# A two-block language-model forward pass: the expert passes' row places in five pieces, and two weight pieces behind the merged rows

## The chip, the cores and the metric

The kernel runs on one core of a Trainium2 chip. The metric is the device time of one execution in microseconds (us). Three runs of the kernel before gave 2496.23, 2499.69 and 2502.55 us; the median is 2499.69 us.

## The reference

The input is 256 tokens of width 1024. Two blocks of two layers each run one after the other, and everything is computed in fp32. In the first block each layer norms the rows, runs four token mixers (retention, a state-space scan, gated linear attention, an mLSTM) on slices of one wide projection, and merges them; then comes a feed-forward part, dense in layer 1 and with eight experts in layer 2. The second block (layers 3 and 4) has other mixers and dense feed-forward parts. Cut to what the change touches:

```
ybr = jnp.stack([y_ret, y_ssd, y_gla, y_ml], axis=2)
gates = jax.nn.sigmoid(mgate.reshape(bsz, seq, N_BRANCH, D_MODEL))
merged = jnp.sum(gates * jnp.einsum('bsnv,nvd->bsnd', ybr, w_branch), axis=2)
return merged @ w_out                       # 1024 x 1024
...
top_vals, top_idx = lax.top_k(logits, TOP_K)          # TOP_K = 2 of 8 experts
...
for e in range(N_EXPERTS):
    out = out + gate[..., e:e + 1] * ((silu(h @ w1[e]) * (h @ w3[e])) @ w2[e])   # 1024 -> 2816 -> 1024
```

## The kernel before, in words

**Weights in two parts.** Every large product is made of three matmuls in a reduced fp32 format: high part of the rows by high part of the weights, low by high, high by low (`split_product`, lines 955 to 957). Weights come by DMA into two ring slots and a third one, on the queue of SyncE. They are then cut into pieces of 128x1024. For each piece ScalarE writes the high part `w_hi` (line 1787, in the experts line 1954), VectorE subtracts it from the weights and writes the low part `w_lo` (line 2811; for the mixers' gate weights GpSimd does it), and TensorE multiplies. There are four places for pieces (`NPIECE`): ScalarE can fill a place when TensorE is done with the piece four before. A ring slot comes free for the next transfer when the low parts of all its pieces are made.

**The order of work.** There is no scheduler. Each engine's program is written out by hand, is executed in that order, and semaphores tie the engines together. An engine that waits holds back all that stands behind it.

**End of the mixers in layers 1 and 2** (`L` 0 and 1). The 1024x1024 output weights are eight pieces, M+40 to M+47, where M is the first piece after the head's. VectorE adds the last gated branch into `merged` (lines 2294 and 2297, eight instructions). TensorE turns the merged rows in four steps into four PSUM banks (line 911), ScalarE copies each to the high part of the rows (`hT_hi`, line 1807), VectorE makes each low part (`low_rows`, in `merged_low`, through line 2811) and with it gives the bank free. The first output product writes one bank per half of the tokens, and these two are the banks of the first two steps: so it starts when two low parts of rows are made. In VectorE's program before, the low parts of pieces M+42 and M+43 stand between the last add and the low parts of the rows.

**The experts** (`experts`). Tokens are sorted to experts, at most 128 to a pass; a pass takes one expert's weights. In this case eight passes run. A pass gathers its rows by matmul, goes through 11 chunks of 256 hidden columns (the loop over `c`, 0 to 11; chunk `c` has four pieces of gate and up weights, and two of the down weights of chunk `c`-1), and the next pass scatters the rows back by a matmul with `selT`. For one chunk VectorE makes six low parts of weights, the low part of the turned hidden rows (`fhT_lo`) and the product of gate and up (line 3020, which the trace calls `u_z`). TensorE's transposes of the hidden rows wait for that product.

At `c` = 1 and 2 VectorE also makes half of the next pass's gather matrix (`select_places`, lines 2949 and 2950). At `c` = 4 it makes all of the scatter matrix and weight of the pass (`places_back`, lines 2999 to 3008): two comparisons of 128x256, their sum, a sum over the row, `selT`, and the next slot number. The trace names their memory `gates`. Each of these waits for the one before it by the semaphore `sel_step`. What it makes is read by the scatter at the start of the next pass.

Of the kernel before, what the change touches and what calls it, by code (L numbers as in the profile page):

```python
# [21 lines left out]
ALU = mybir.AluOpType  # L22
ACT = mybir.ActivationFunctionType
AX = mybir.AxisListType

P = 128
STEP, LINE = 8, 16
T = 2
# [131 lines left out]
HEAD_PIECES = sum(CHUNK_PIECES[:6])  # L160
# [97 lines left out]
def build(nc, a, out):  # L258
# [7 lines left out]
    with ctx:  # L266
# [10 lines left out]
        def sem(name):  # L277
            return ctx.enter_context(nc.semaphore(name))
# [32 lines left out]
        with ExitStack() as expert_rows:  # L311
            selT = expert_rows.enter_context(nc.sbuf_tensor("selT", [P, S], F32R))
# [82 lines left out]
        slot_no, slot_weight = g1[:, 324:325], g1[:, 325:326]  # L395
        quad_b = g0[:, 0:4 * S].rearrange("p (q s) -> p q s", q=4)
        sel = g0[:, 4 * S:5 * S].rearrange("p (t s) -> p t s", t=T)
        slot_rows, slot_rows2 = g0[:, 5 * S:6 * S], g0[:, 6 * S:7 * S]
# [6 lines left out]
        def const2(name):  # L405
# [70 lines left out]
        both_ready, count_mm, rank_mm, quad_ready, quad_out, quad_in, table_ready = (sem(s) for s in (  # L476
            "both_ready", "count_mm", "rank_mm", "quad_ready", "quad_out", "quad_in", "table_ready"))
        sel_ready, gather_mm, xg_ready, selT_ready, scatter_mm, ys_ready = (sem(s) for s in (
            "sel_ready", "gather_mm", "xg_ready", "selT_ready", "scatter_mm", "ys_ready"))
# [33 lines left out]
        MIX, FFN = [0] * 4, [0] * 3  # L513
# [16 lines left out]
        for key, m in PC.of.items():  # L530
            if key[0] != "ffn" and key[:-1] + (key[-1] + 1,) not in PC.of:
                L, job = key[0], key[1:-1]
# [114 lines left out]
        for l in range(2):  # L647
            L = 2 + l
# [1498 lines left out]
        def _(v):  # L2147
            tt, ts, stt, cp = nc.vector.tensor_tensor, nc.vector.tensor_scalar, nc.vector.scalar_tensor_tensor, nc.vector.tensor_copy
# [197 lines left out]
            def mixers(L):  # L2346
# [12 lines left out]
                M = M0 + HEAD_PIECES  # L2359
# [23 lines left out]
                for n in range(4):  # L2383
# [4 lines left out]
                         in1=ea[:, L].unsqueeze(1).to_broadcast([P, T, 4]), op0=ALU.mult, op1=ALU.mult))  # L2388
# [114 lines left out]
                head_norm(L, 3, 2, u_gla[:, :, 4 + MW:], False)  # L2503
                low_range(M + 40, M + 42)
                merge(L, 3)
                low_range(M + 42, M + 44)

            def normed(src, n_g, cols, gcol, m, r, w):

# [300 lines left out]
            def low(dst, src, hi):  # L2810
                return tt(dst, src, hi.bitcast(F32), ALU.subtract)  # L2811

            def low_range(lo, hi):

                for m in range(lo, hi):
                    v.wait_ge(w_hi_ready, m + 1)
                    low(w_lo[:, m % NPIECE], source[m][0], w_hi[:, m % NPIECE]).then_inc(w_split, 1)
# [128 lines left out]
            def select_places(step, tiles=range(T)):  # L2946

                for i in tiles:
                    step(ts(sel[:, i], const("iota"), place[:, 0, i:i + 1], None, ALU.is_equal))
                    ins = stt(out=sel[:, i], in0=const("iota"), scalar=place[:, 1, i:i + 1], in1=sel[:, i], op0=ALU.is_equal, op1=ALU.add)  # L2950
                    if i < T - 1:
                        step(ins)
                    else:
                        ins.then_inc(sel_ready, 1)

            def experts():
                route()
                select_places(link)
                pass_table()
                n_pass = passes(v)  # L2960

                def rows_low(passed):

                    for h in range(2):
                        cols = slice(h * 512, (h + 1) * 512)
                        v.wait_ge(ys_hi_ready, 2 * passed + h + 1)
                        ins = stt(out=ys_lo[:, cols], in0=mb[h][:], scalar=slot_weight, in1=ys_hi[:, cols].bitcast(F32),
                                  op0=ALU.mult, op1=ALU.subtract)
                    ins.then_inc(ys_ready, 1)

                with v.Fori(0, n_pass) as t:
                    n = [0]
                    STEPS = 9

                    def step(ins):
                        n[0] += 1
                        ins.then_inc(sel_step, 1)
                        v.wait_ge(sel_step, t * STEPS + n[0])

                    def low_parts(lo, hi):  # L2980
                        for m in range(lo, hi):
                            c, q = PIECE_LIST[m]
                            v.wait_ge(e_hi_ready, t * ALL_PIECES + m + 1)
                            low(w_lo[:, m % NPIECE], expert_piece(c, q), w_hi[:, m % NPIECE]).then_inc(e_split, 1)

                    def gathered(half):
                        v.wait_ge(xg_hi_ready, 2 * t + half + 1)
                        low(xg_lo[:, 4 * half:4 * half + 4], mb[2 + half][:].rearrange("p (k s) -> p k s", k=4),
                            xg_hi[:, 4 * half:4 * half + 4]).then_inc(xg_ready, 1)

                    at = 4
                    low_parts(0, 1)
                    gathered(0)
                    low_parts(1, 2)
                    gathered(1)
                    low_parts(2, 4)
                    rows_low(t)

                    def places_back():
                        v.wait_ge(quad_in, 16)  # L3000
                        v.wait_ge(scatter_mm, T * (t + 1))
                        step(stt(out=slot_rows, in0=quad_b[:, 0], scalar=slot_no, in1=quad_b[:, 2], op0=ALU.is_equal, op1=ALU.mult))
                        step(stt(out=slot_rows2, in0=quad_b[:, 1], scalar=slot_no, in1=quad_b[:, 3], op0=ALU.is_equal, op1=ALU.mult))
                        step(tt(slot_rows, slot_rows, slot_rows2, ALU.add))
                        step(nc.vector.tensor_reduce(slot_weight, slot_rows, AX.X, ALU.add))
                        ts(selT[:], slot_rows, 0.0, None, ALU.is_gt).then_inc(selT_ready, 1)
                        v.wait_ge(selT_ready, t + 2)
                        step(ts(slot_no, slot_no, float(P), None, ALU.add))

                    for c in range(NF + 1):  # L3010
                        if c:
                            low_parts(at, min(pieces(c) + 3, ALL_PIECES))
                            at = min(pieces(c) + 3, ALL_PIECES)
                            v.wait_ge(e_ht_hi, t * NF + c)
                            low(fhT_lo[:, :, 0:P], mb[3][:, 0:2 * P].rearrange("p (k s) -> p k s", k=2), fhT_hi[:, :, 0:P]).then_inc(e_ht, 1)
                        if c < NF:
                            low_parts(at, pieces(c + 1) + 1)
                            at = pieces(c + 1) + 1
                            v.wait_ge(e_silu, t * NF + c + 1)
                            tt(fh[:, 0, :], fsg[:, 0, :], mb[2][:, FC:2 * FC], ALU.mult).then_inc(e_h, 1)  # L3020
                        if c == 0:
                            v.wait_ge(sel_ready, t + 1)
                            qv = place.rearrange("p q t -> p (q t)")
                            step(ts(qv, qv, -float(P), None, ALU.add))
                        if c == 1 or c == 2:
                            select_places(step, (c - 1,))
                        if c == 4:
                            places_back()
                assert n[0] == STEPS, n[0]
                rows_low(n_pass)  # L3030
                final_and_first(lambda i: (scatter_mm, n_pass * T + (1 + i)))

            for L in range(2):
                norm(2 * L)
                mixers(L)
                merged_low(L)
                low_range(MIX[L] + HEAD_PIECES + 44, MIX[L] + HEAD_PIECES + 48)
                add_out(L, 0)
                if L == 0:
                    low_parts(0, 0, 1)  # L3040
                    low_turned(0, 0, 0)
                    low_turned(0, 0, 1)
                    low_parts(0, 1, 2)
                    add_out(0, 1)
                    ts(t_out, rstd, 1.0, None, ALU.mult).then_inc(xn_ready, T)
                    ffn(0)
                else:
                    add_out(1, 1)
                    v.wait_ge(squares, T * 4)
                    link(ts(r_in, ssq, ROOT_SCALE / D, ROOT_SCALE * EPS, ALU.mult, ALU.add))  # L3050
                    rsqrt(rstd, r_in)
                    for i in range(T):
                        ts(xn[:, i, :], merged[:, i, :], rstd[:, i:i + 1], None, ALU.mult).then_inc(xn_ready, 1)
                    experts()
            for l in range(2):
                L, n = 2 + l, 5 + 4 * l
# [30 lines left out]
```

## Time and profile before

| what | before |
|---|---|
| runs, median of 3 | 2499.69 us (2496.23 to 2502.55) |
| the profiled execution, its own time | 2488.17 us |
| its span | 2486.3 us |
| mean granted TensorE clock, share of full speed | 0.984 |
| TensorE matmul busy | 2386.1 us (96%) |
| TensorE weight load busy | 1950.4 us (78%) |
| VectorE busy | 1718.9 us (69%) |
| ScalarE busy | 1383.9 us (56%) |
| GpSimd busy | 410.7 us (17%) |
| HBM read | 547.43 MB, 221 GB/s over the span |

In the profile, PE is TensorE's matmuls, PEld its weight loads, DVE VectorE, ACT ScalarE, POOL GpSimd, SP the queue of SyncE. An instruction's idle time is that of its engine just before it, with what ended the wait. The span is 2486.3 us long: the mixers of layer 1 end near 277 us, those of layer 2 near 762 us, and the expert passes lie between 812 and 1611 us.

### The profile page before, as it was taken

What the parts mean: (1) busy time and instruction counts of PE and PEld (TensorE: products, weight loads), DVE (VectorE), ACT (ScalarE), POOL (GpSimd) and SP (SyncE); (2) the same over time, 40 slices, a digit from 0 to 9 for tenths busy, and PEclk for the clock granted to TensorE, in tenths of its full rate; (3) what the DMA queues carried; (4) which work ended last, traced back from release to release, by engine and by line L of the source; (5) the groups of instructions that cost most, each with busy time, mean ns of one, the idle gap of its engine ahead of it and who ended that gap; (6) DMA issues with size and microseconds to landing.
All of it is one profiled execution on the core that took longest, in us unless ns stands there. A gap on an engine that the chain in (4) does not pass through costs nothing.

```text
span 2486.3 us, 31992 instructions
## 1 busy us (share of the span) xinstructions
PE 2386.1 (96%) x11841; PEld 1950.4 (78%) x11841; DVE 1718.9 (69%) x2295; ACT 1383.9 (56%) x1753; POOL 410.7 (17%) x229
## 2 busy tenths in 40 slices
PE   7999999999998999999999999999999989998998
PEld 6986688798766788888888888777768878776886
DVE  4847655566585889889899898884565557346555
ACT  4544354445432788878878888655344444534443
POOL 2146000002540000000000000065600007550000
PEclk9999999999998999999999999999999999999999
DMA  7434575344335899999999999854475634447560
GB/s 230 170 119 159 172 245 185 105 141 156 136 136 186 292 340 368 336 336 367 338 337 367 338 367 338 290 158 145 152 245 187 203 112 138 140 164 240 171 203 34
DMA packets 381876, 549.91 MB, mean 221 GB/s; under 512 B 27268, under 2 KB 283640, under 8 KB 381640
## 3 DMA queue, kind: packets, MB, share of 16 engines
q1 hardware_dynamic: 377392, 535.82, 63.4%
q0 software_dynamic: 4096, 12.11, 1.8%
q8 instruction: 69, 1.13, 0.2%
q10 hardware_dynamic: 288, 0.59, 0.1%
q14 instruction: 31, 0.25, 0.0%
HBM read 547.43 MB, written 1.05 MB: 221 GB/s over the span
## 4 chain that ended last, share of the span: by engine, by line
PE 81%; DVE 11%; DMA 3%; ACT 2%; issue 2%; POOL 0%; SPq 0%; DVEq 0%; ACTq 0%
PE mb L955 13%; PE mb L957 13%; PE mb L956 13%; PE pb L955 9%; PE pb L957 9%; PE pb L956 9%; DMA ring<-in_w_in 2%; PE pb L1474 2%; DVE w_lo L2811 2%; PE pb L1075 1%; PE mb L1341 1%; DMA down_w<-in_moe_w 1%; PE pb L1419 1%; PE mb L1102 1%; DVE merged L2297 1%
## 5 line engine op out<-in xcount | busy, mean ns | idle before, releaser
L2811 DVE TENSOR_TENSOR w_lo<-ring,w_hi 128x1024 fp32r<-128x1024 f32 x444 | 534.8, 1222 | 215.9 <-ACT w_hi L1787 169.3
L800 POOL TENSOR_TENSOR w_lo<-ring,w_hi 128x1024 fp32r<-128x1024 f32 x152 | 372.1, 2475 | 1425.2 <-DVE xn L2641 807.7
L1787 ACT ACTIVATE w_hi<-ring 128x1024 fp32r<-128x1024 f32 x340 | 348.6, 1054 | 297.1 <-PE pb L957 125.5
L955 PE MATMUL mb<-w_hi,hT_hi 128*128 128x512 f32 x1232 | 493.0, 400 | 8.7 <-DVE w_lo L2811 7.2
L957 PE MATMUL mb<-w_lo,hT_hi 128*128 128x512 f32 x1232 | 481.6, 391 | 0.0
L955 PE MATMUL pb<-w_hi,hT_hi 128*128 128x512 f32 (+1 forms) x928 | 354.2, 382 | 10.7 <-DVE low_rows L2811 6.3
L2811 DVE TENSOR_TENSOR w_lo<-down_w,w_hi 128x1024 fp32r<-128x1024 f32 x242 | 293.9, 1223 | 86.8 <-ACT w_hi L1787 79.3
L957 PE MATMUL pb<-w_lo,hT_hi 128*128 128x512 f32 (+1 forms) x928 | 345.4, 372 | 0.0
L956 PE MATMUL pb<-w_hi,low_rows 128*128 128x512 f32 (+1 forms) x928 | 345.3, 372 | 0.0
L1954 ACT ACTIVATE w_hi<-ring 128x1024 fp32r<-128x1024 f32 x256 | 269.1, 1058 | 26.1 <-PE mb L957 23.8
L955 PEld LDWEIGHTS mb<-w_hi,hT_hi 128*128 128x128 f32 x1232 | 231.8, 188 | 59.4 <-DVE w_lo L2811 13.4
L956 PE MATMUL mb<-w_hi,xg_lo 128*128 128x512 f32 x704 | 274.7, 390 | 0.0
L957 PEld LDWEIGHTS mb<-w_lo,hT_hi 128*128 128x128 f32 x1232 | 231.7, 188 | 49.7
L955 PEld LDWEIGHTS pb<-w_hi,hT_hi 128*128 128x128 f32 x928 | 178.4, 192 | 45.1 <-DVE low_rows L2811 6.4
L1954 ACT ACTIVATE w_hi<-down_w 128x1024 fp32r<-128x1024 f32 x176 | 186.9, 1062 | 40.2 <-PE mb L957 36.0
L956 PE MATMUL mb<-w_hi,low_rows 128*128 128x512 f32 x528 | 206.3, 391 | 0.0
L957 PEld LDWEIGHTS pb<-w_lo,hT_hi 128*128 128x128 f32 x928 | 178.2, 192 | 30.4
L956 PEld LDWEIGHTS pb<-w_hi,low_rows 128*128 128x128 f32 x928 | 178.4, 192 | 28.5 <-issue 1.0
L2811 DVE TENSOR_TENSOR w_lo<-third_gu,w_hi 128x1024 fp32r<-128x1024 f32 x132 | 159.4, 1223 | 38.7 <-ACT w_hi L1787 30.6
L956 PEld LDWEIGHTS mb<-w_hi,xg_lo 128*128 128x128 f32 x704 | 132.6, 188 | 24.6
L955 PE MATMUL mb<-w_hi,fhT_hi 128*128 128x512 f32 x352 | 137.6, 391 | 0.0
L957 PE MATMUL mb<-w_lo,fhT_hi 128*128 128x512 f32 x352 | 137.3, 390 | 0.0
(492 smaller groups left out, 3607.7 us busy)
## 6 DMA issues: line engine op xcount, KB each, us to landing
ring<-in_moe_w SPq DMA_DIRECT2D x128, 1024.0 KB, 9.1
ring<-in_w_in SPq DMA_DIRECT2D x50, 2048.0 KB, 8.0
down_w<-in_moe_w SPq DMA_DIRECT2D x88, 1024.0 KB, 12.1
third_gu<-in_moe_w SPq DMA_DIRECT2D x48, 1024.0 KB, 10.8
down_w<-in_w_ffn_down SPq DMA_DIRECT2D x22, 1024.0 KB, 9.9
ring<-in_w_out SPq DMA_DIRECT2D x8, 2048.0 KB, 8.2
ring<-in_ffn_w SPq DMA_DIRECT2D x16, 1024.0 KB, 8.0
ring<-in_w_ffn_gate SPq DMA_DIRECT2D x16, 1024.0 KB, 5.5
```

The costliest lines, as they stand in the source:

```text
L800: nc.gpsimd.tensor_tensor(w_lo[:, m % NPIECE], source[m][0], w_hi[:, m % NPIECE].bitcast(F32), ALU.subtract).then_inc(pool_split, 1)
L955: mm(o, a_hi, hi, start=start, stop=False)
L956: mm(o, a_lo, hi, start=False, stop=False)
L957: return mm(o, a_hi, lo, start=False, stop=stop)
L1075: ins = mm(bank[:], yT[:, b % 2, kk, i * P:(i + 1) * P], w[:, kk, h * 512:(h + 1) * 512], start=kk == 0, stop=kk == 1)
L1102: ins = mm(banks[i][:, h * w:(h + 1) * w], probs[:, h, at:at + P], v(j, h), start=n == 0, stop=n == len(parts) - 1)
L1341: ins = mm(mb[2 + half][:, (k % 4) * P:(k % 4 + 1) * P], xn[:, i, k * P:(k + 1) * P], sel[:, i], start=i == 0, stop=i == T - 1)
L1419: ins = mm(bank[:, 0:n], hT[:, k, i * P:(i + 1) * P], wv[:, k], start=k == 0, stop=k == KD - 1)
L1474: ins = mm(bank[:], src[:, kk, i * P:(i + 1) * P], w[:, kk, h * 512:(h + 1) * 512], start=kk == 0, stop=kk == n_k - 1)
L1787: f(w_hi[:, m % NPIECE], src, ACT.Copy).then_inc(w_hi_ready, 1)
L1954: f(w_hi[:, n % NPIECE], expert_piece(c, q), ACT.Copy).then_inc(e_hi_ready, 1)
L2811: return tt(dst, src, hi.bitcast(F32), ALU.subtract)
```

## The change

Two edits. In `experts`, `places_back` takes the chunk's number and makes one piece of its work after each of the chunks 4 to 8, with the same instructions and the same waits in the same order. In the mixers of layers 1 and 2, the low parts of the pieces M+42 and M+43 are made after `merged_low` and not before it.

```diff
@@ the mixers of layers 1 and 2, VectorE
                 head_norm(L, 3, 2, u_gla[:, :, 4 + MW:], False)
                 low_range(M + 40, M + 42)
                 merge(L, 3)
-                low_range(M + 42, M + 44)
@@ experts, VectorE
-                    def places_back():
-                        v.wait_ge(quad_in, 16)
-                        v.wait_ge(scatter_mm, T * (t + 1))
-                        step(stt(out=slot_rows, in0=quad_b[:, 0], scalar=slot_no, in1=quad_b[:, 2], op0=ALU.is_equal, op1=ALU.mult))
-                        step(stt(out=slot_rows2, in0=quad_b[:, 1], scalar=slot_no, in1=quad_b[:, 3], op0=ALU.is_equal, op1=ALU.mult))
-                        step(tt(slot_rows, slot_rows, slot_rows2, ALU.add))
-                        step(nc.vector.tensor_reduce(slot_weight, slot_rows, AX.X, ALU.add))
-                        ts(selT[:], slot_rows, 0.0, None, ALU.is_gt).then_inc(selT_ready, 1)
-                        v.wait_ge(selT_ready, t + 2)
-                        step(ts(slot_no, slot_no, float(P), None, ALU.add))
+                    def places_back(c):
+                        if c == 4:
+                            v.wait_ge(quad_in, 16)
+                            v.wait_ge(scatter_mm, T * (t + 1))
+                            step(stt(out=slot_rows, in0=quad_b[:, 0], scalar=slot_no, in1=quad_b[:, 2], op0=ALU.is_equal, op1=ALU.mult))
+                        elif c == 5:
+                            step(stt(out=slot_rows2, in0=quad_b[:, 1], scalar=slot_no, in1=quad_b[:, 3], op0=ALU.is_equal, op1=ALU.mult))
+                        elif c == 6:
+                            step(tt(slot_rows, slot_rows, slot_rows2, ALU.add))
+                        elif c == 7:
+                            step(nc.vector.tensor_reduce(slot_weight, slot_rows, AX.X, ALU.add))
+                        else:
+                            ts(selT[:], slot_rows, 0.0, None, ALU.is_gt).then_inc(selT_ready, 1)
+                            v.wait_ge(selT_ready, t + 2)
+                            step(ts(slot_no, slot_no, float(P), None, ALU.add))
...
-                        if c == 4:
-                            places_back()
+                        if 4 <= c <= 8:
+                            places_back(c)
@@ after the mixers of layers 1 and 2, VectorE
                 mixers(L)
                 merged_low(L)
-                low_range(MIX[L] + HEAD_PIECES + 44, MIX[L] + HEAD_PIECES + 48)
+                low_range(MIX[L] + HEAD_PIECES + 42, MIX[L] + HEAD_PIECES + 48)
                 add_out(L, 0)
```

Only VectorE's program changes. Line numbers of the changed kernel differ by one after line 2506 and by four after `places_back`.

VectorE in layer 1, from the last add into `merged` to the first output sums, before:

```order
L2294 TENSOR_TENSOR gates<-pb,gates 128x512
L2297 TENSOR_TENSOR merged<-merged,gates 128x512
L2811 TENSOR_TENSOR w_lo<-ring,w_hi 128x1024 x2
L2811 TENSOR_TENSOR low_rows<-pb,hT_hi 128x2x256 x4
L2811 TENSOR_TENSOR w_lo<-ring,w_hi 128x1024 x4
L2803 TENSOR_TENSOR x<-x,pb 128x512 x2
```

and in the changed kernel:

```order
L2294 TENSOR_TENSOR gates<-pb,gates 128x512
L2297 TENSOR_TENSOR merged<-merged,gates 128x512
L2810 TENSOR_TENSOR low_rows<-pb,hT_hi 128x2x256 x4
L2810 TENSOR_TENSOR w_lo<-ring,w_hi 128x1024 x6
L2802 TENSOR_TENSOR x<-x,pb 128x512 x2
L2806 TENSOR_TENSOR merged<-x,gain 128x512 x2
```

The two low parts of weights that stood ahead of the four low parts of rows stand behind them; layer 2 reads the same.

VectorE in an expert pass, from the product of chunk 4 to the next low parts of weights, before (the REGISTER_ALU rows prepare the value that a wait compares with):

```order
L3020 TENSOR_TENSOR u_z<-xs,mb 128x256
L3001 REGISTER_ALU
L3002 SCALAR_TENSOR_TENSOR gates<-gates 128x256
L2978 REGISTER_ALU
L3003 SCALAR_TENSOR_TENSOR gates<-gates 128x256
...
L3004 TENSOR_TENSOR gates<-gates 128x256
...
L3005 TENSOR_REDUCE gates<-gates 128x1
...
L3006 TENSOR_SCALAR selT<-gates 128x256
L3007 REGISTER_ALU
L3008 TENSOR_SCALAR gates<-gates 128x1
...
L2811 TENSOR_TENSOR w_lo<-third_gu,w_hi 128x1024
```

and in the changed kernel, from the product of chunk 4 to behind that of chunk 5:

```order
L3024 TENSOR_TENSOR u_z<-xs,mb 128x256
L3001 REGISTER_ALU
L3002 SCALAR_TENSOR_TENSOR gates<-gates 128x256
L2977 REGISTER_ALU
L2982 REGISTER_ALU
L2810 TENSOR_TENSOR w_lo<-third_gu,w_hi 128x1024
...
L2810 TENSOR_TENSOR fhT_lo<-mb,fhT_hi 128x2x128
...
L3024 TENSOR_TENSOR u_z<-xs,mb 128x256
L3004 SCALAR_TENSOR_TENSOR gates<-gates 128x256
```

One of the six instructions stays at chunk 4; the second follows the product of chunk 5, and the others those of chunks 6, 7 and 8, the last two together.

## Rows read from the trace of the kernel before

**Rows 1.** The page's first part: busy time of each engine.
```profile
PE 2386.1 (96%) x11841; PEld 1950.4 (78%) x11841; DVE 1718.9 (69%) x2295; ACT 1383.9 (56%) x1753; POOL 410.7 (17%) x229
```

**Rows 2.** Waits of PE, 820 to 1620 us: total us, times, longest.
```profile
PE mb L955 <- DVE w_lo L2811: 7.2, 8, 1.9
```

**Rows 3.** Timeline of DVE, pass 4, chunk 4: start us, us, instruction, idle before.
```profile
1152.46 0.41 DVE L3020 TENSOR_TENSOR u_z<-xs,mb 128x256 f32<-128x256 f32 x1
1152.79 0.48 DVE L3002 SCALAR_TENSOR_TENSOR gates<-gates 128x256 f32<-128x256 f32 x1
...
1153.83 0.43 DVE L3004 TENSOR_TENSOR gates<-gates 128x256 f32<-128x256 f32 x1
...
1154.74 0.29 DVE L3006 TENSOR_SCALAR selT<-gates 128x256 fp32r<-128x256 f32 x1
1155.07 0.16 DVE L3008 TENSOR_SCALAR gates<-gates 128x1 f32<-128x1 f32 x1
1155.35 2.36 DVE L2811 TENSOR_TENSOR w_lo<-third_gu,w_hi 128x1024 fp32r<-128x1024 f32 x2
```

**Rows 4.** Timeline of PE, passes 1 and 4: the matmul after the wait.
```profile
858.51 0.50 PE L955 MATMUL mb<-w_hi,hT_hi 128*128 128x512 f32 x1 [1.87 <-DVE w_lo L2811]
...
1156.63 0.49 PE L955 MATMUL mb<-w_hi,hT_hi 128*128 128x512 f32 x1 [0.75 <-DVE w_lo L2811]
```

**Rows 5.** Timeline of DVE, pass 4: a full chunk behind the wait, and one while it catches up.
```profile
1157.63 0.42 DVE L2811 TENSOR_TENSOR fhT_lo<-mb,fhT_hi 128x256 fp32r<-128x256 f32 x1
...
1165.10 0.42 DVE L2811 TENSOR_TENSOR fhT_lo<-mb,fhT_hi 128x256 fp32r<-128x256 f32 x1
...
1170.35 0.41 DVE L3020 TENSOR_TENSOR u_z<-xs,mb 128x256 f32<-128x256 f32 x1
...
1173.78 1.23 DVE L2811 TENSOR_TENSOR w_lo<-ring,w_hi 128x1024 fp32r<-128x1024 f32 x1 [0.25 <-ACT w_hi L1954]
...
1178.76 0.41 DVE L3020 TENSOR_TENSOR u_z<-xs,mb 128x256 f32<-128x256 f32 x1
```

**Rows 6.** Timeline of DVE, pass 4, chunk 2: the gather places.
```profile
1135.97 0.28 DVE L2949 TENSOR_SCALAR gates<-cst,gates 128x128 f32<-128x128 f32 x1
1136.29 0.35 DVE L2950 SCALAR_TENSOR_TENSOR gates<-cst,gates 128x128 f32<-128x128 f32 x1
```

**Rows 7.** Timeline of ACT, pass 1: waits for the weights' DMA, at chunks 5 and 10.
```profile
852.11 1.06 ACT L1954 ACTIVATE w_hi<-third_gu 128x1024 fp32r<-128x1024 f32 x1 [1.57 <-DMA down_w<-in_moe_w]
...
895.35 1.06 ACT L1954 ACTIVATE w_hi<-ring 128x1024 fp32r<-128x1024 f32 x1 [0.39 <-DMA down_w<-in_moe_w]
```

**Rows 8.** Windows in pass 4: length, busy PE, PEld, DVE, ACT, POOL, clock, DMA share, GB/s.
```profile
1158.00:1166.00 8.00, 8.00 (x38) 6.58 (x37) 8.00 (x10) 6.46 (x8) 0.00 (x0) 1.00 1.08 368
...
1198.00:1206.00 8.00, 8.00 (x39) 6.60 (x38) 7.14 (x8) 5.51 (x7) 0.00 (x0) 1.00 0.77 242
```

**Rows 9.** Timeline of PE, end of the mixers of layer 1.
```profile
277.39 1.06 PE L911 MATMUL pb<-cst,merged 128*128 128x128 f32 x8 [0.83 <-DVE merged L2297]
280.98 0.47 PE L955 MATMUL pb<-w_hi,hT_hi 128*128 128x512 f32 x1 [2.52 <-DVE low_rows L2811]
```

**Rows 10.** Timeline of DVE, the same stretch.
```profile
276.56 0.69 DVE L2297 TENSOR_TENSOR merged<-merged,gates 128x512 f32<-128x512 f32 x1
277.17 2.35 DVE L2811 TENSOR_TENSOR w_lo<-ring,w_hi 128x1024 fp32r<-128x1024 f32 x2
279.44 2.48 DVE L2811 TENSOR_TENSOR low_rows<-pb,hT_hi 128x512 fp32r<-128x512 f32 x4
```

**Rows 11.** Timeline of ACT, the same stretch.
```profile
276.17 1.08 ACT L1807 ACTIVATE hT_hi<-pb 128x512 fp32r<-128x512 f32 x2 [5.79 <-PE pb L911]
278.06 1.09 ACT L1807 ACTIVATE hT_hi<-pb 128x512 fp32r<-128x512 f32 x2 [0.81 <-PE pb L911]
```

**Rows 12.** Windows at the start of the output product, layer 1; columns as in group 8.
```profile
281.00:284.65 3.65, 3.65 (x10) 2.85 (x10) 0.91 (x2) 0.00 (x0) 0.00 (x0) 0.54 1.07 378
284.65:288.30 3.65, 3.65 (x17) 3.01 (x16) 1.23 (x1) 1.06 (x1) 0.00 (x0) 0.99 1.10 348
```

**Rows 13.** Waits of PE, 757 to 830 us (layer 2): total us, times, longest.
```profile
PE pb L955 <- DVE low_rows L2811: 2.5, 1, 2.5
```

## The prediction

> **What bounds the kernel now.** The page's busy times come first: TensorE's matmuls fill 96% of the span, VectorE is at 69% [rows 1]. So time is won where TensorE waits, and little else counts. Next come TensorE's waits, by stretch. In the expert passes there is one kind that matters: eight waits for a low part of weights, 7.2 us in all, the longest 1.9 [rows 2], one a pass. At the end of the mixers of layers 1 and 2 TensorE waits 2.5 us for the low parts of the merged rows [rows 9, 13]. Last, the timelines of VectorE and ScalarE there show what stands in the way, and the windows show the granted clock and the DMA engines.
>
> **First edit: the row places.** Nothing is added or removed. Six instructions of each pass, with their waits, leave one place and stand at five.
>
> - What the block costs now. In pass 4 it starts at 1152.79 and the next low part of weights at 1155.35, 2.56 us later [rows 3]. That low part is the second piece of chunk 5, and TensorE gets it at 1156.63 after 0.75 us of waiting [rows 4]. So TensorE's lead covers 2.56 - 0.75 = 1.8 us of lateness there, and only the rest is paid. In pass 1 it is 1.87 us [rows 4].
> - What the changed block costs there. One comparison stays: from 1152.79 to the next one's start it is 0.52 us (0.48 and a short wait; the third instruction starts two such intervals later, at 1153.83). 0.52 is far below the 1.8 that are covered, so the wait goes: 7.2 us over eight passes.
> - What the other four pieces cost. They are 0.52, two of together 0.91 (1153.83 to 1154.74), and for the last two instructions 1155.35 - 1154.74 = 0.61 us, one piece per chunk [rows 3]. VectorE needs 8.41 us for a chunk when it follows TensorE (1170.35 to 1178.76), of which 0.25 is one visible wait; while it catches up it does a chunk in 7.47 us (1157.63 to 1165.10) [rows 5]. So 0.94 us of each chunk is slack, more than any piece. The nearest like case is already in the kernel: at chunks 1 and 2 the gather places take 0.28 and 0.35 us with a gap [rows 6], in two chunks running, and the waits of the passes are the eight of group 2 alone, so none is there. I cost the four pieces at nothing, under cover of that slack; without it the 2.04 us of a pass would all be paid. Nobody waits for their results before the scatter of the next pass.
> - What is late next: the weights. A chunk is three transfers of 1024x256 fp32 values, and from chunk 5 to chunk 10 of pass 1 the arrivals for which ScalarE waits lie (895.35 - 852.11) / 5 = 8.65 us apart [rows 7] against TensorE's 8.41. In pass 1 ScalarE was late by 1.57 us at chunk 5 and by 0.39 at chunk 10. If TensorE runs 1.87 us ahead, it is late by 2.26 at chunk 10. A lateness of 1.57 was borne before, so I take 2.26 - 1.57 = 0.7 us as a new wait and 1.2 as pass 1's gain. In the later passes the DMA engines are full in the middle and at 0.77 at the end of a pass [rows 8], so they recover each time. There TensorE comes only 0.75 us sooner, which is under the 1.57 that pass 1 shows as harmless. Transfers start when a slot's low parts are made, up to 0.6 us later than now, but other transfers are queued ahead of them.
> - Sum of the edit: 7.2 - 0.7 = 6.5 us.
>
> **Second edit: two low parts of weights.** Layer 1; layer 2 has the same wait to a tenth of a us [rows 9, 13].
>
> - Removed from ahead of the rows: two low parts, which start at 277.17 and put the rows' first one to 279.44, 2.27 us [rows 10]. ScalarE has the first two high parts of rows done at 276.17 + 1.08 = 277.25 [rows 11], just when the last add ends (276.56 + 0.69). So VectorE can start at once, and the first two low parts of rows are made at about 277.25 + 1.24 = 278.5, plus the 0.25 us that now lie between them and TensorE's start: 278.7 in place of 280.98. TensorE's own transposes end at 277.39 + 1.06 = 278.45 [rows 9] and are no bound. Gain 2.27 us a layer, 4.5 in two.
> - Added behind: the third and fourth low parts of rows wait for ScalarE (278.06 + 1.09 = 279.15) [rows 11] and are made by 279.9; then the two moved pieces, at 1.18 us each, by 281.1 and 282.3. TensorE wants them after two and three groups of twelve matmuls. At full clock a matmul is 0.23 us (3.65 us for some 16) [rows 12], so that is 278.7 + 5.5 = 284.2 and 286.9. There is room of 3 us, so cost nothing. The slot of these weights comes free 2.8 us later, for a transfer that is first used at the start of the feed-forward part more than 8 us on; nothing.
> - The clock. TensorE's granted clock is 0.54 over the 3.65 us from the start of the output product, and 0.99 in the next 3.65 [rows 12]: it fell to 1.2 GHz behind the 2.52 us of idleness. Some nine matmuls instead of 16 run there, which costs 3.65 x 0.46 = 1.7 us. With 0.25 us of idleness in place of 2.52, I take it that the clock stays at 2.4 GHz: 1.7 us a layer, 3.4 in two. The bounds are nothing (it falls as now) and 3.4; a wait of 1.87 us in pass 1 [rows 4] left the clock at full, and this is nearer to what will be left.
>
> The Trainium skill speaks against this last term. "TensorE: Matmul & The Clock Gate", in "A second HAM failure mode: psum-queue depth-cycling", says that small idle times between groups of matmuls can be enough for the clock to go down and up again. Here the transposes and their 0.83 us gap remain, so by it the clock could fall as before and the sum would be 11.0 instead of 14.4. The trace bears it out only in part: the fall comes after the long idleness and not after the 0.83 us.
>
> **The sum.** 6.5 + 4.5 + 3.4 = 14.4 us. The profiled execution took 2488.17 us (span 2486.3) and would take 2473.8. It lies 11.5 us under the median of the runs, 2499.69; I carry the difference over: 2499.69 - 14.4 = 2485.3 us. A difference of 0.3% is 7.5 us, about what a measurement of this kernel can tell from none.
>
> **Rivals.**
>
> - *The clock falls anyway*, at the output product or on the transposes ahead of it. For it: a 0.83 us wait and transposes stay just ahead [rows 9]. Against it: they stand there now, at full clock. Gain 6.5 + 4.5 = 11.0, 2488.7 us. In one layer only: 12.7.
> - *The passes gain nothing*, since transfers or the scattered pieces take the wait over. For it: DMA engines are full from the start to chunk 10, and VectorE is busy for 8.00 of the 8 us after the block [rows 8]. Against it: the idle DMA share at each pass's end, and the gather places that cost nothing. Gain 4.5 + 3.4 = 7.9, 2491.8 us.
> - *Slower: VectorE's slack isn't usable.* If the 0.94 us per chunk are handshakes that a piece can't fill, each of the five pieces reaches TensorE in full, 2.56 us a pass: 8 x 2.56 - 7.2 = 13.3 us lost. Less 7.9 for the second edit that is 5.4 us slower, 2505.1, and 8.8 slower if the clock falls as well. It decides from the point at which a chunk's slack is under 0.5 us. The catch-up chunk of 7.47 us [rows 5] speaks against it.
> - *The second edit does not do what it says*, because something else holds the output product: ScalarE's copies would, but they end at 277.25. Then only 6.5 us are won, 2493.2.
>
> **How the numbers follow.** Forecast 0.60; clock 0.20; passes gain nothing 0.10; second edit void 0.05; slower 0.05, of which 0.03 beyond 7.5 us. The likeliest, 2485.3, is given. The range goes from 2480 (the forecast, with 1.7 us more from a clock fall avoided elsewhere and the runs' scatter of 3 us) to 2494 (the last gaining rival). Faster by over 0.3% are the forecast, the clock rival and half of the third case, 0.85; within 0.3% the rest, 0.12; slower 0.03.
>
> **What would show it.** Right: no wait for a low part of weights at chunk 5 in any pass, at most one short one near chunk 10 of pass 1; each pass from the second on shorter by about 0.75 us; VectorE's low parts of rows directly behind the last add; TensorE's wait of 2.52 us down to about 0.25; granted clock 1.00 at the start of both output products. Wrong: waits of TensorE in chunks 6 to 9, ScalarE waiting for DMA in passes 3 to 8, or a clock near 0.5 behind the transposes.

## The result, and the profile after

| | before | changed kernel |
|---|---|---|
| median of 8 runs | 2493.09 us (2483.54 to 2502.55) | 2478.20 us (2472.04 to 2485.02) |
| profiled execution | 2488.17 us | 2478.46 us |
| its span | 2486.3 us | 2476.7 us |

The ratio is 0.9939, with a 95% interval of 0.9922 to 0.9956: about 15.2 us of 2493 (11.0 to 19.4). The medians differ by 14.9 us. The forecast was 14.4, so the change is faster by about what was said; but the time, 2478.20, lies below the range, which began at 2480. More runs of the kernel before have moved its median from 2499.69 (3 runs) to 2493.09.

First the page's busy times of the changed kernel, which answer to [rows 1]. TensorE has as much work as before, in a shorter span.

```profile
span 2476.7 us, 31992 instructions
PE 2387.6 (96%) x11841; PEld 1952.3 (79%) x11841; DVE 1707.9 (69%) x2295; ACT 1381.6 (56%) x1753; POOL 411.0 (17%) x229
```

TensorE's waits from 830 to 1620 us (us in total, times, longest), which answer to [rows 2]. The row of 7.2 us in eight waits for `w_lo` is gone; what is left stands behind the last pass.

```profile
PE pb L1409 <- DVE xn L2640: 6.3, 1, 6.3
PE pb L1353 <- DVE ys_lo L2966: 0.6, 1, 0.6
```

VectorE in pass 4, behind the products of chunks 4 and 5 (start us, us, instruction), which answers to [rows 3]. Only one comparison stands between `u_z` and the low parts of weights: they start 0.60 us after that comparison starts, where it was 2.56.

```profile
1142.24 0.48 DVE L3002 SCALAR_TENSOR_TENSOR gates<-gates 128x256 f32<-128x256 f32 x1
1142.84 2.36 DVE L2810 TENSOR_TENSOR w_lo<-third_gu,w_hi 128x1024 fp32r<-128x1024 f32 x2
...
1150.65 0.48 DVE L3004 SCALAR_TENSOR_TENSOR gates<-gates 128x256 f32<-128x256 f32 x1
1151.25 2.36 DVE L2810 TENSOR_TENSOR w_lo<-ring,w_hi 128x1024 fp32r<-128x1024 f32 x2
```

TensorE at the end of the mixers of layers 1 and 2, which answers to [rows 9, 13]. The wait for the low parts of the rows is 0.24 us, not 2.52, in both layers.

```profile
275.56 1.06 PE L911 MATMUL pb<-cst,merged 128*128 128x128 f32 x8 [0.82 <-DVE merged L2297]
276.87 0.47 PE L955 MATMUL pb<-w_hi,hT_hi 128*128 128x512 f32 x1 [0.24 <-DVE low_rows L2810]
...
759.31 0.47 PE L955 MATMUL pb<-w_hi,hT_hi 128*128 128x512 f32 x1 [0.24 <-DVE low_rows L2810]
```

VectorE in layer 1, against [rows 10]: the rows' low parts come straight behind the last add, and then the moved low parts of weights.

```profile
274.72 0.69 DVE L2297 TENSOR_TENSOR merged<-merged,gates 128x512 f32<-128x512 f32 x1
275.33 1.28 DVE L2810 TENSOR_TENSOR low_rows<-pb,hT_hi 128x512 fp32r<-128x512 f32 x2
276.86 1.29 DVE L2810 TENSOR_TENSOR low_rows<-pb,hT_hi 128x512 fp32r<-128x512 f32 x2 [0.24 <-ACT hT_hi L1807]
278.06 2.35 DVE L2810 TENSOR_TENSOR w_lo<-ring,w_hi 128x1024 fp32r<-128x1024 f32 x2
```

The window of 3.65 us from the start of that product, with the columns of [rows 8], answers to [rows 12]: granted clock 1.00, 16 matmuls where 10 ran.

```profile
276.87:280.52 3.65, 3.65 (x16) 3.02 (x17) 3.54 (x4) 0.44 (x1) 0.00 (x0) 1.00 1.05 401
```

The price of the passes is read on VectorE between the first `ys_lo`, at the start of pass 1, and the last one, behind pass 8. From one `ys_lo` to the next is the period of a pass. Before:

```profile
817.37 1.40 DVE L2967 SCALAR_TENSOR_TENSOR ys_lo<-mb,gates,ys_hi 128x512 fp32r<-128x512 f32 x2
...
917.98 1.40 DVE L2967 SCALAR_TENSOR_TENSOR ys_lo<-mb,gates,ys_hi 128x512 fp32r<-128x512 f32 x2
...
1116.75 1.40 DVE L2967 SCALAR_TENSOR_TENSOR ys_lo<-mb,gates,ys_hi 128x512 fp32r<-128x512 f32 x2
...
1608.72 1.41 DVE L2967 SCALAR_TENSOR_TENSOR ys_lo<-mb,gates,ys_hi 128x512 fp32r<-128x512 f32 x2 [4.50 <-ACT ys_hi L1945]
```

and the changed kernel:

```profile
809.98 1.40 DVE L2966 SCALAR_TENSOR_TENSOR ys_lo<-mb,gates,ys_hi 128x512 fp32r<-128x512 f32 x2
...
909.47 1.40 DVE L2966 SCALAR_TENSOR_TENSOR ys_lo<-mb,gates,ys_hi 128x512 fp32r<-128x512 f32 x2
...
1106.16 1.40 DVE L2966 SCALAR_TENSOR_TENSOR ys_lo<-mb,gates,ys_hi 128x512 fp32r<-128x512 f32 x2
...
1592.99 1.41 DVE L2966 SCALAR_TENSOR_TENSOR ys_lo<-mb,gates,ys_hi 128x512 fp32r<-128x512 f32 x2 [4.50 <-ACT ys_hi L1945]
```

From first to last it is 791.35 us before and 783.01 after, so the passes are 8.3 us shorter. Pass 1 gave 100.61 - 99.49 = 1.1 us of it, and each later one about 1.03 (from 1116.75 to 1608.72 against 1106.16 to 1592.99 it is 5.14 us in five).

The end of the passes comes 15.7 us sooner (1608.72 against 1592.99), the end of the span only 9.6. The 6.1 us were lost in layers 3 and 4, whose code the change does not touch. Two windows of 100 us there, of the same work, show where: the granted clock. Before:

```profile
2000.00:2100.00 100.00, 92.21 (x500) 76.21 (x499) 67.56 (x106) 44.09 (x64) 37.07 (x22) 0.97 0.42 130
2210.00:2310.00 100.00, 92.49 (x387) 68.71 (x386) 56.65 (x87) 40.16 (x56) 21.26 (x10) 0.97 0.61 210
```

After:

```profile
1984.30:2084.30 100.00, 92.21 (x474) 74.91 (x473) 59.35 (x107) 44.47 (x65) 32.31 (x20) 0.95 0.41 129
2194.30:2294.30 100.00, 93.36 (x389) 69.14 (x388) 54.14 (x88) 40.74 (x58) 21.28 (x10) 0.95 0.63 221
```

A window's granted clock gives its time at 1.2 GHz (0.97 over 100 us is 6 us of it). Added up over windows of 10 us, from the last `ys_lo` to the end of the span there are 34 us at 1.2 GHz before and 51 after. Such a stretch costs up to half its length, so 17 us more of it cover the 6.1. Whether the change causes this or the executions differ was a question for the experiments.

### The profile page after: what moved, and what is told of

The parts are those of the page before. It is cut to its first block, busy times and chain, and to the rows that moved or that the text cites. A ratio compares the mean times of both kernels' runs of the same rounds, so it can differ in the third digit from the quotient of the medians.

```text
span 2476.7 us, 31992 instructions
## 1 busy us (share of the span) xinstructions
PE 2387.6 (96%) x11841; PEld 1952.3 (79%) x11841; DVE 1707.9 (69%) x2295; ACT 1381.6 (56%) x1753; POOL 411.0 (17%) x229
## 4 chain that ended last, share of the span: by engine, by line
PE 85%; DVE 10%; DMA 2%; ACT 2%; issue 1%; SPq 0%; ACTq 0%; DVEq 0%
PE mb L955 15%; PE mb L957 15%; PE mb L956 15%; PE pb L955 9%; PE pb L957 8%; PE pb L956 8%; PE pb L1474 2%; DMA ring<-in_w_in 2%; PE pb L1075 1%; DVE w_lo L2810 1%; PE mb L1341 1%; PE pb L1419 1%; DVE merged L2297 1%; PE mb L1102 1%; DVE conv L2214 1%
## 5 line engine op out<-in xcount | busy, mean ns | idle before, releaser
L1954 ACT ACTIVATE w_hi<-down_w 128x1024 fp32r<-128x1024 f32 x176 | 187.1, 1063 | 31.4 <-PE mb L957 27.2
L2810 DVE TENSOR_TENSOR w_lo<-third_gu,w_hi 128x1024 fp32r<-128x1024 f32 x132 | 159.3, 1221 | 37.6 <-ACT w_hi L1787 30.6
```

The source lines that it names most:

```text
L1954: f(w_hi[:, n % NPIECE], expert_piece(c, q), ACT.Copy).then_inc(e_hi_ready, 1)
```

## The experiments

Three theories were open. That the sum is right: the eight waits, the two waits at the output products, and the clock behind them. That the forecast's base was off, since three runs gave it. And as a rival, that the change pushes the clock down in layers 3 and 4 and so gives some of its gain back. Against each theory stood its parts alone, the kernels repeated, and VectorE's slack measured by itself. The first three kernels below, and that with two chunks, were timed beside the kernel before, whose 28 runs there have a median of 2493.01 us (2483.25 to 2502.05). The other four kernels (the kernel before again, one piece behind the rows, the doubled and the tripled pieces) have one run each, beside one of the kernel before with 2488.45 us; they are read from their traces, and their times alone decide little.

### The first edit alone

The second edit is undone in the changed kernel:

```diff
                 merge(L, 3)
+                low_range(M + 42, M + 44)
@@
-                low_range(MIX[L] + HEAD_PIECES + 42, MIX[L] + HEAD_PIECES + 48)
+                low_range(MIX[L] + HEAD_PIECES + 44, MIX[L] + HEAD_PIECES + 48)
```

> The first edit alone. The theory (both edits count, and add): no wait of TensorE for a low part of weights in any pass, 7.2 us won there and about 7 to 8 us over the whole kernel (ratio 0.997), while the 2.5 us waits at the two output products of layers 1 and 2 stay, with the clock near 0.54 behind them. The rival, that the passes gain nothing since the weights' DMA takes the wait over: no change, ratio 1.000, and TensorE's eight waits come back as waits for late weights in chunks 6 to 10.

Measured: 2484.23 us (12 runs, 2480.32 to 2490.90), ratio 0.9964 with 0.9947 to 0.9980, about 9.0 us faster than before (5.0 to 13.2). There is no wait for `w_lo` in the passes, and from the first `ys_lo` to the last it takes 8.2 us less:

```profile
824.70 1.40 DVE L2967 SCALAR_TENSOR_TENSOR ys_lo<-mb,gates,ys_hi 128x512 fp32r<-128x512 f32 x2
...
1607.84 1.41 DVE L2967 SCALAR_TENSOR_TENSOR ys_lo<-mb,gates,ys_hi 128x512 fp32r<-128x512 f32 x2 [4.50 <-ACT ys_hi L1945]
```

It also shows pass 1 under late weights. These are three turns of `u_z` on TensorE, one a chunk, in the middle of pass 1: they lie 8.7 us apart, where a chunk of the later passes takes 8.41 [rows 5], and no wait is listed.

```profile
870.85 0.38 PE L1372 MATMUL mb<-cst,u_z 128*128 128x128 f32 x2
...
879.56 0.44 PE L1372 MATMUL mb<-cst,u_z 128*128 128x128 f32 x2
...
888.28 0.44 PE L1372 MATMUL mb<-cst,u_z 128*128 128x128 f32 x2
```

The output products keep their waits of 2.52 us, and in both layers the clock is low behind them (windows of 3.65 us, columns as in [rows 8]):

```profile
283.69:287.34 3.65, 3.65 (x10) 2.91 (x11) 0.93 (x2) 0.00 (x0) 0.00 (x0) 0.60 1.05 377
770.53:774.18 3.65, 3.65 (x9) 2.88 (x10) 0.94 (x2) 0.00 (x0) 0.00 (x0) 0.50 1.06 332
```

What follows: the first edit works as described. The passes are 8.2 us shorter and the runs 9.0 us (5.0 to 13.2), where the sum had 6.5.

### The second edit alone

In the kernel before:

```diff
                 merge(L, 3)
-                low_range(M + 42, M + 44)
@@
-                low_range(MIX[L] + HEAD_PIECES + 44, MIX[L] + HEAD_PIECES + 48)
+                low_range(MIX[L] + HEAD_PIECES + 42, MIX[L] + HEAD_PIECES + 48)
```

> The second edit alone. The theory: the eight waits of the passes stay (7.2 us), the two waits of 2.5 us fall to about 0.25, and the granted clock is 1.00 over the start of both output products; 4.5 us from the waits and 3.4 from the clock, 7.9 us in all (ratio 0.997). The rival, that the clock falls for another reason than the idleness: 4.5 us alone, ratio 0.998, and a clock near 0.5 somewhere in the first 4 us of the output products.

Measured: 2490.45 us (12 runs, 2480.86 to 2494.75), ratio 0.9978 with 0.9960 to 0.9996, about 5.5 us faster (1.0 to 10.0). Both output products start behind 0.24 us of waiting, at full clock. The passes' waits stand as before:

```profile
PE mb L955 <- DVE w_lo L2810: 7.1, 8, 1.9
```

The two edits alone add up to 9.0 + 5.5 = 14.5 us, and together they give 15.2: they are independent, within what is measured. The 5.5 lies between 4.5 and 7.9, the sum of this edit without and with the clock's term, and its interval does not tell the two apart. From the last `ys_lo` on, this kernel's profile holds 51 us at 1.2 GHz, as the changed kernel's does.

### The changed kernel again

No edit.

> The changed kernel once more. The theory, that its profiled execution lost some 5 us in layers 3 and 4 (code that the change doesn't touch) to stretches of low clock that fall differently from one execution to the next: the waits at the two output products are again about 0.25 us and the passes again free of waits, but the stretches of low clock in layers 3 and 4 sum to another length than in the first profile, by several us; ratio 0.993 to 0.995. The rival, that the change itself brings those stretches about: the same extra low clock in layers 3 and 4 again.

Measured: 2479.43 us (7 runs, 2473.01 to 2482.44), ratio 0.9944 with 0.9921 to 0.9966, about 14.0 us. The first result repeats, and so does the time of the kernel before, 2493 in 28 runs. The base of 2499.69 was 6.7 us too high. The waits are as expected: 0.25 us at both output products, none in the passes. The clock is not: the theory wanted another length of low clock in layers 3 and 4, and from the last `ys_lo` on this profile again holds 51 us at 1.2 GHz. That is what the rival said.

The runs list the mean granted clock of each execution, and this weighs more than single profiles. The 28 runs of the kernel before have a mean of 0.9817, the 15 of the changed kernel (8 and 7) 0.9821: the change costs no clock over the whole span. The clock also orders the runs. Of the kernel before, the two at 0.986 took 2483.25 and 2484.09 us, the three at 0.978 took 2499.79 to 2500.47. Straight lines of one slope through the 77 runs of five kernels (before, changed, each edit alone, two chunks), each kernel's at its own height, give 0.42 us for each us more at 1.2 GHz, and as differences at equal clock 13.2 us for the change, 7.8 for the first edit and 4.7 for the second, each to about 1.1 us. These are estimates; they lie near what the waits gave back, 8.3 and 4.6.

### The kernel before again

No edit, one run.

> The kernel before, profiled once more. Theory (stretches of low clock in layers 3 and 4 depend on how the work falls against a grid of clock decisions that is placed anew in each execution): another sum of low clock in layers 3 and 4 than the 27.2 us of the first profile is possible, up to the 44.2 us that the kernels with the second edit show, and the two 2.5 us waits are again followed by low clock. Rival (the second edit brings the extra 17 us of low clock about): 27 us again.

Measured: 2491.45 us, 3.3 above the first profile of this kernel. From the last `ys_lo` on it holds 44 us at 1.2 GHz where the first profile has 34, in the same program: 10 of the 17 us between before and after are seen without the change. The rival wanted the same sum again. (The expectation's 27.2 and 44.2 us count a shorter stretch, without the start of this one.) At the output products the expectation missed. Both waits of 2.5 us are there, and behind neither did the clock fall:

```profile
283.11 0.47 PE L955 MATMUL pb<-w_hi,hT_hi 128*128 128x512 f32 x1 [2.51 <-DVE low_rows L2811]
...
767.78 0.47 PE L955 MATMUL pb<-w_hi,hT_hi 128*128 128x512 f32 x1 [2.52 <-DVE low_rows L2811]
```

```profile
283.11:286.76 3.65, 3.65 (x16) 3.06 (x17) 0.95 (x2) 0.58 (x1) 0.00 (x0) 1.00 1.06 377
767.78:771.43 3.65, 3.65 (x16) 3.02 (x17) 0.94 (x2) 0.00 (x0) 0.00 (x0) 1.00 1.06 334
```

So the 2.52 us are followed by a low clock in four of six stretches (two here, two of the kernel before, two of the first edit alone), not each time. The term of 3.4 us is what is won when it would have fallen twice.

### One piece behind the rows

Half of the second edit: M+42 stays ahead of the merged rows, and M+43 goes behind them.

```diff
                 merge(L, 3)
+                low_range(M + 42, M + 43)
@@
-                low_range(MIX[L] + HEAD_PIECES + 42, MIX[L] + HEAD_PIECES + 48)
+                low_range(MIX[L] + HEAD_PIECES + 43, MIX[L] + HEAD_PIECES + 48)
```

> As the changed kernel, but only one of the two low parts (M+43) stands behind the low parts of the rows. Theory: TensorE waits about 0.25 + 1.13 = 1.4 us at each output product of layers 1 and 2 in place of 0.25, and the clock stays full there, since the 1.87 us wait in the passes did not lower it either. Rival: the clock falls as behind 2.5 us, near 0.55 over the next 3.7 us.

Measured: 2484.28 us in one run. The wait is 1.38 us in both layers, and the clock is full behind both:

```profile
281.02 0.47 PE L955 MATMUL pb<-w_hi,hT_hi 128*128 128x512 f32 x1 [1.38 <-DVE low_rows L2811]
```

```profile
281.02:284.67 3.65, 3.65 (x16) 3.05 (x17) 2.08 (x3) 0.11 (x1) 0.00 (x0) 1.00 0.89 325
764.68:768.33 3.65, 3.65 (x16) 3.06 (x17) 2.07 (x3) 0.00 (x0) 0.00 (x0) 1.00 1.04 345
```

A piece moved is 1.14 us of waiting removed. In all profiles with a wait of 1.4 us or less at this place, seven of them with 14 stretches, the clock was full.

### Two chunks instead of five

The six instructions stand at chunks 4 and 5, three each: 1.5 us in one block.

```diff
                         if c == 4:
...
-                        elif c == 5:
                             step(stt(out=slot_rows2, in0=quad_b[:, 1], scalar=slot_no, in1=quad_b[:, 3], op0=ALU.is_equal, op1=ALU.mult))
-                        elif c == 6:
                             step(tt(slot_rows, slot_rows, slot_rows2, ALU.add))
-                        elif c == 7:
+                        else:
                             step(nc.vector.tensor_reduce(slot_weight, slot_rows, AX.X, ALU.add))
-                        else:
                             ts(selT[:], slot_rows, 0.0, None, ALU.is_gt).then_inc(selT_ready, 1)
@@
-                        if 4 <= c <= 8:
+                        if 4 <= c <= 5:
```

> As the changed kernel, but the row places are made in two portions: three instructions at chunk 4 (1.5 us) and three at chunk 5 (1.06 us). The theory (TensorE's lead covers up to 1.8 us of lateness of one block): no wait in the passes, the same time as the changed kernel within 1 us. The rival, that only pieces below a chunk's own slack of 0.94 us are free: 1.5 - 0.94 = 0.6 us of waiting a pass comes back, 4 to 5 us slower than the changed kernel.

Measured: 2479.47 us (10 runs, 2472.07 to 2488.09), ratio 0.9945 with 0.9923 to 0.9967: the same as the changed kernel. One wait for `w_lo` came back, in pass 1, where the weights are late as well:

```profile
849.89 0.50 PE L955 MATMUL mb<-w_hi,hT_hi 128*128 128x512 f32 x1 [0.89 <-DVE w_lo L2810]
```

That is near the 1.5 us less the lead that pass 1 had, 2.56 - 1.87 = 0.69. In the other seven passes no wait is listed, as the lead of 1.8 us says, but each takes 98.5 us where the changed kernel takes 98.3. From the first `ys_lo` to the last it is 784.64 us against 783.01: two chunks give back 1.6 of the 8.3 us, too little for the runs to tell. The rival's 4 to 5 us did not come, so most of the gain needs only a block below the lead.

### The pieces doubled, and tripled

Each of the chunks 4 to 8 gets one further comparison, in the second kernel two, which write the same values to `slot_rows2` once more. For chunk 4, with n of 1 or 2 (`STEPS` grows by 5n, and the other chunks get the same lines):

```diff
                             step(stt(out=slot_rows, in0=quad_b[:, 0], scalar=slot_no, in1=quad_b[:, 2], op0=ALU.is_equal, op1=ALU.mult))
+                            for _ in range(n):
+                                step(stt(out=slot_rows2, in0=quad_b[:, 1], scalar=slot_no, in1=quad_b[:, 3], op0=ALU.is_equal, op1=ALU.mult))
```

> As the changed kernel, with one more comparison of 128x256 after each of the chunks 4 to 8 (a repeat, its result is not used): each chunk's portion is about 1.0 to 1.1 us in place of 0.5. Theory (a chunk has 0.94 us of slack and TensorE's lead covers 1.8 us): the portions pile up to 5 x 0.1 us only, no wait in passes 2 to 8. Rival (the slack is not usable and the pieces' 2.5 us are just under what the lead covers): 5.1 us a pass against 1.8, some 3 us of waits in each pass.

Measured: 2473.40 us, one run. In the passes two waits are left, both short and both in pass 1:

```profile
PE mb L1372 <- DVE u_z L3033: 0.5, 1, 0.5
PE mb L955 <- DVE w_lo L2810: 0.4, 1, 0.4
```

So about 1.0 us in each of five chunks, twice what the change puts there, is still hidden but for a rest; the pass period is 98.55 us against the changed kernel's 98.30, and the eight passes take 785.47 us against 783.01, 2.5 more. That this run is 5 us below the changed kernel's median is no gain of the added work: its whole span holds 71 us at 1.2 GHz, against 95 in the changed kernel's profile, and 2473.4 lies within that kernel's own runs.

> As the changed kernel, with two more comparisons of 128x256 after each of the chunks 4 to 8 (repeats, their results are not used): each portion is about 1.55 us. Theory: the portions exceed the slack of 0.94 us by 0.6 each, 3.1 us over five chunks, of which the lead covers 1.8; waits of about 1.3 us a pass come back, in chunks 7 to 9 and not at chunk 5, 10 us in all. Rival (no usable slack): 7.7 us a pass less 1.8, some 6 us of waits a pass, 47 us in all.

Measured: 2500.56 us. TensorE's waits from 830 to 1630 us:

```profile
PE mb L955 <- DVE w_lo L2810: 13.0, 33, 1.0
```

In pass 4 they stand in chunks 6 to 9, two of them here:

```profile
1167.03 0.50 PE L955 MATMUL mb<-w_hi,hT_hi 128*128 128x512 f32 x1 [0.40 <-DVE w_lo L2810]
...
1176.10 0.50 PE L955 MATMUL mb<-w_hi,hT_hi 128*128 128x512 f32 x1 [0.35 <-DVE w_lo L2810]
```

VectorE's portion in that chunk, and the low parts of weights behind it:

```profile
1173.23 0.42 DVE L3009 TENSOR_TENSOR gates<-gates 128x256 f32<-128x256 f32 x1
1173.69 1.01 DVE L3011 SCALAR_TENSOR_TENSOR gates<-gates 128x256 f32<-128x256 f32 x2
1174.82 2.36 DVE L2810 TENSOR_TENSOR w_lo<-ring,w_hi 128x1024 fp32r<-128x1024 f32 x2
```

A chunk takes 1176.10 - 1167.03 = 9.07 us there. That is VectorE's catch-up chunk of 7.47 us [rows 5] and the portion of 1.59 (1174.82 - 1173.23): TensorE is now paced by VectorE, and 9.07 - 8.41 = 0.66 us of each such chunk is paid. The pass period is 101.16 us, 2.86 over the changed kernel's 98.30, and the eight passes take 806.72 us, 23.7 more; the listed waits show 13.0 of it. The expectation of 10 us, in chunks 7 to 9, was too small by its own means. It took the lead of 1.8 us as spent late, but the portion in chunk 4 uses most of it at once, so with portions of 1.55 us and a slack of 0.94 it had to be 1.55 + 4 x 0.61 - 1.8 = 2.2 us a pass. The rest to 2.86 stays open. The rival, no usable slack, wanted 47 us and is out.

## Why the prediction was right, and where it was wrong

**The step that failed** is the last of the sum: "I carry the difference over: 2499.69 - 14.4 = 2485.3 us." The base was a median of three runs, and 28 later ones of the same kernel have 2493.01; from that base the forecast would be 2478.6, and 2478.20 was measured. The difference, 14.4 against 14.9 to 15.2, came out near, in part by luck: the passes were priced 1.8 us too low and the clock at least 1.1 too high. The profiled execution, 2488.17, lay 11.5 us below that base; the text gave this gap and took nothing from it. The runs show what the gap is made of: that execution had a mean clock of 0.984, the three at that clock among the 28 took 2485.29 to 2489.76 us, and times like those of the base are found at 0.978 to 0.981. (The clocks of the base's own three runs are not on record.) The range had the same fault: it gave "the runs' scatter of 3 us", half of the three runs' spread, where 28 runs spread over 19. Carried from the profiled execution, the forecast would be 2473.8, and a range for both bases begins there or below.

**Eight waits: right in place, too small in price.** They are gone, as said, and the other pieces cost nothing. But the 7.2 us of idleness cost more than 7.2. TensorE in pass 4 of the kernel before, around the wait of [rows 4]:

```profile
1155.26 0.40 PE L956 MATMUL mb<-w_hi,xg_lo 128*128 128x512 f32 x1
1155.49 0.40 PE L957 MATMUL mb<-w_lo,hT_hi 128*128 128x512 f32 x1
...
1156.96 0.39 PE L956 MATMUL mb<-w_hi,xg_lo 128*128 128x512 f32 x1
```

A matmul is shown as 0.40 us long, but the next one starts 0.23 us behind it. From 1155.49 to 1156.63, where the wait ends, it is 1.14 us, and 0.33 more to the next one at 1156.96: 1.47 us for what else takes 0.46. So the wait costs 1.01 us, and its row says 0.75. The periods of passes 4 to 8 give 1.03. Seven passes at 1.03 and pass 1 with 1.1 make the 8.3 us.

**Late weights: right.** Pass 1 gained 1.1 us where 1.2 were forecast. ScalarE's waits for DMA from 812 to 1000 us grew to

```profile
ACT w_hi L1954 <- DMA down_w<-in_moe_w: 16.6, 15, 1.6
```

and end with pass 2. The form was not as forecast: no wait of TensorE near chunk 10, but chunks of 8.7 us instead of 8.41, in gaps too small for the view of waits. Before, they were 2.9 us in four waits. No later pass has such waits, so the 0.77 of the DMA engines at a pass's end [rows 8] was read rightly.

**The output products: right.** 2.52 to 0.24 us, twice: 4.6 us against 4.5.

**The clock: right at the two products, not shown as a gain of the whole.** It was full at both products in every kernel with the second edit. The Trainium skill's "TensorE: Matmul & The Clock Gate", in "A second HAM failure mode: psum-queue depth-cycling", tells of a kernel in which small idle times between groups of matmuls made the clock go down and up. At this place no run shows that: the transposes and their 0.82 us of waiting stayed, and the clock did not fall in 14 of 14 stretches. But the loss that was priced at 1.7 us a layer occurs in four of six stretches with the long wait, so its mean worth is at most some two thirds of 3.4, or 2.3 us. That share comes from six stretches and is rough. Nor is it shown that the time is kept: between the first transposes of layer 1 and the first `ys_lo` the profile before holds 37.6 us at 1.2 GHz and the profile after 37.7, so what did not fall at the products fell elsewhere, and the mean clock of the second edit's 12 runs, 0.9814, is not above the 0.9817 of the kernel before. What is shown is 8.3 + 4.6 = 12.9 us. With the 2.3 it would be 15.2; the interval of the result, 11.0 to 19.4, does not choose, and the 13.2 at equal clock leaves the clock out by its making.

**The rivals.** All four fell. The clock stays up at both products; the passes do gain; the second edit does what it says; and VectorE's slack is usable, since doubled pieces cost 0.3 us a pass and tripled ones 2.9. The point from which slack decides was named rightly in kind: a portion beyond 0.94 us a chunk, for which the lead of 1.8 us stands in for a few chunks. The rival that came up with the result, that the change lowers the clock in layers 3 and 4, does not hold for the whole span, as the runs' mean clocks show, but for those layers it is not settled. From the last `ys_lo` on, the profiles without the second edit have 34, 34 (the first edit alone) and 44 us at 1.2 GHz. The changed kernel has 51 twice, the second edit alone 51, two chunks 51, one piece behind 46. Against the rival stand the two kernels that keep both edits and have longer pieces, with 34 each. The windows of the doubled pieces, of the same work as those of the result, read as the kernel before:

```profile
1985.00:2085.00 100.00, 92.21 (x499) 76.16 (x498) 67.52 (x106) 44.10 (x64) 36.84 (x22) 0.97 0.42 129
2195.00:2295.00 100.00, 92.46 (x386) 68.72 (x385) 56.34 (x88) 40.24 (x57) 21.24 (x10) 0.97 0.61 210
```

What sets the number of these stretches in one execution stays open. That it differs between executions of one program is shown, by 34 against 44 us in the kernel before.

## What to carry to other kernels

Work on an engine with slack should be cut to less than the slack between two of its deadlines plus the lead that the waiting engine has: here, with 1.8 us of lead and 0.94 us a chunk, 1.5 us in one block cost 1.6 us over the eight passes and 1.0 us in each of five chunks 2.5, and the next step up cost 24. Price a stall by the distance between the starts of the instructions around it, not by the idle time that its row shows. And where a forecast is a time, its base needs as much care as its difference: look at the granted clock of the profiled execution, set its time against a median of few runs, and where they lie 11 us apart, let the range reach to both.

## What the runs showed of the hardware that was not expected

- The granted clock's answer to an idle time is not fixed: after 2.52 us it was 0.50 to 0.60 over the next 3.65 us in four stretches and 1.00 in two, and the kernel before shows both. After 0.24 to 1.4 us it was 1.00 in all 14.
- One kernel's runs spread over 19 us, and their mean granted clock goes with it: 0.986 at 2483 and 2484 us, 0.978 at 2500. Profiles of it and of its near relatives hold 71 to 100 us at 1.2 GHz in the whole span, and the two profiles of the kernel before differ by 17 us in this and by 3.3 us in time.
- A resource that is 3% too slow, the weights' DMA in pass 1 with 8.7 us a chunk against 8.41, shows in no wait of TensorE at all, only in the distances between its turns.
